# Three stage borders of a hybrid encoder layer: a GpSimd wait, a store on another queue, a regrouped gate product and a later awaited store

## What is computed

```
hn = rms_norm(h, norm_w);  proj = hn @ w_in          # qa ka va za, gates, qb kb vb zb, qc zc
qkv = silu(centred_depthwise_conv([qa, ka, va], conv_w_a)); qa, ka = l2_norm(qa), l2_norm(ka)
o_fwd = gated_delta_rule_chunked(qa, ka, va, g_f, bt_f)
o_bwd = flip(gated_delta_rule_chunked(flip(qa), flip(ka), flip(va), flip(g_b), flip(bt_b)))
o_a = rms_norm(o_fwd + o_bwd, o_norm_a) * silu(za)   # per head of 128
o_b = windowed_gqa_with_sink(rope(rms_norm(qb)), rope(rms_norm(kb)), vb, sink) * silu(zb)
o_c = memory_cross_attention(rms_norm(qc), rms_norm(km), vm) * silu(zc)
return h + concat(o_a, o_b, o_c) @ w_out
```

## Time and profile before

| | us |
|---|---|
| median of 3 runs | 2324.76 |
| lowest and highest of them | 2321.35, 2329.73 |
| profiled execution, its own time | 2328.26 |
| its span in the trace | 2326.6 |
| TensorE busy | 2164.2 (93% of the span) |
| VectorE, ScalarE, GpSimd busy | 1083.9, 660.8, 314.1 |
| front stage, until TensorE's last instruction in it | 1197.2 |
| delta stage, until the engines start the next | 1787.2 |
| attention stage, until SyncE's first load of the next | 1953.6 |
| output stage, until the end of the span | 2326.6 |
| mean granted TensorE clock | 0.97 of full speed |

### The profile page before, as it was taken

The page is one execution under the profiler, slowest core; times in us unless marked ns, Lnnn a source line. Parts: engine busy times, 40 slices in busy tenths (PEclk is TensorE's granted clock), DMA queues, the critical chain, the costliest instruction groups (busy, mean ns, idle before and its releaser), DMA issues. The chain is left out here.

```text
span 2326.6 us, 28431 instructions
## 1 busy us (share of the span) xinstructions
PE 2164.2 (93%) x11264; PEld 1807.5 (78%) x11264; DVE 1083.9 (47%) x1854; ACT 660.8 (28%) x1004; POOL 314.1 (13%) x195
## 2 busy tenths in 40 slices
PE   6999999999999999999967999999987785999998
PEld 6888888888888888888856888888885454888887
DVE  7764444444444311221318666666644876323222
ACT  6511111111111110111115454444433665211110
POOL 4300000000000000000005444455401000000000
PEclk9999999999999999999988999999979997999999
DMA  6522122122122212212121221111111125534432
GB/s 225 191 85 81 55 81 81 54 81 81 55 81 81 81 58 78 81 54 81 46 84 55 81 93 58 64 64 64 46 64 55 55 82 184 214 127 149 158 126 90
DMA packets 78866, 210.87 MB, mean 91 GB/s; under 512 B 7328, under 2 KB 33056, under 8 KB 74560
## 3 DMA queue, kind: packets, MB, share of 16 engines
q1 hardware_dynamic: 69088, 174.04, 22.5%
q0 software_dynamic: 9696, 35.72, 3.9%
HBM read 165.11 MB, written 44.63 MB: 90 GB/s over the span
## 5 line engine op out<-in xcount | busy, mean ns | idle before, releaser
L73 PE MATMUL pr_acc<-x_hi,pr_w_lo 128*128 128x512 f32 (+1 forms) x1760 | 675.8, 384 | 26.4 <-DVE pr_w_lo L431 20.7
L74 PE MATMUL pr_acc<-x_lo,pr_w_hi 128*128 128x512 f32 (+1 forms) x1760 | 674.1, 383 | 0.0
L75 PE MATMUL pr_acc<-x_hi,pr_w_hi 128*128 128x512 f32 (+1 forms) x1760 | 674.0, 383 | 0.0
L73 PEld LDWEIGHTS pr_acc<-x_hi,pr_w_lo 128*128 128x128 f32 x1760 | 334.0, 190 | 91.9 <-issue 18.7
L74 PEld LDWEIGHTS pr_acc<-x_lo,pr_w_hi 128*128 128x128 f32 x1760 | 334.1, 190 | 63.8 <-issue 0.2
L75 PEld LDWEIGHTS pr_acc<-x_hi,pr_w_hi 128*128 128x128 f32 x1760 | 334.1, 190 | 63.4
L347 ACT ACTIVATE pr_w_hi<-pr_w_raw 128x1024 fp32r<-128x1024 f32 x118 | 124.9, 1060 | 749.3 <-PE pr_acc L75 728.4
L532 DVE TENSOR_TENSOR pr_padded<-pr_acc,pr_rstd 128x512 f32<-128x512 f32 x82 | 56.6, 692 | 518.4 <-PE pr_acc L75 518.3
L73 PE MATMUL ou_acc<-ou_w_hi,ou_m_lo 128*128 128x512 f32 x512 | 200.5, 392 | 18.1 <-DVE ou_w_lo L1842 18.1
L74 PE MATMUL ou_acc<-ou_w_lo,ou_m_hi 128*128 128x512 f32 x512 | 200.4, 391 | 0.0
L75 PE MATMUL ou_acc<-ou_w_hi,ou_m_hi 128*128 128x512 f32 x512 | 200.1, 391 | 0.0
(11 more groups left out here) (240 smaller groups left out, 2508.1 us busy)
## 6 DMA issues: line engine op xcount, KB each, us to landing
pr_w_raw<-in_w_in SPq DMA_DIRECT2D x118, 512.0 KB, 5.1
ou_w_raw<-in_w_out SPq DMA_DIRECT2D x32, 1024.0 KB, 4.9
proj_scratch<-pr_res POOLq DMA_DIRECT2D x50, 512.0 KB, 5.2
dl_qk<-proj_scratch SPq DMA_DIRECT2D x8, 1024.0 KB, 5.0
dl_grow<-gate_rows SPq DMA_DIRECT2D x8, 1024.0 KB, 7.6
ou_x_in<-in_x SPq DMA_DIRECT2D x8, 1024.0 KB, 7.1
out<-ou_res POOLq DMA_DIRECT2D x8, 1024.0 KB, 4.7
pr_res<-in_x_t SPq DMA_DIRECT2D x11, 512.0 KB, 5.9
```

Of the source, the lines that this page charges most:

```text
L73: pe.matmul(out, w_lo, x_hi, start=first, stop=False)
L74: pe.matmul(out, w_hi, x_lo, start=False, stop=False)
L75: return pe.matmul(out, w_hi, x_hi, start=False, stop=last)
```

## The change

It has five parts.

1. GpSimd no longer issues the store of the last projection tile. SyncE does, after the two stores of gate rows; GpSimd waits only until that tile has been taken, then goes to the border.
2. In the delta stage GpSimd waits for `e_d1` of 4, VectorE's four products and sums of head 0 (L1129 and L1135), before `decayed_queries(0)`.
3. In the slot of head 7, ScalarE does the squares of the attention keys and of the first two tiles (`early_squares`) right after the squares of head 6, ahead of that head's roots. Before they came behind them.
4. After the delta stage's last exponential for the attention stage, ScalarE takes one logarithm of a single column into `negc`, which nobody reads.
5. For head 7, VectorE multiplies `po`, `onorm` and `z` as soon as the squares are taken (two operations), and the root is applied in one last operation. `fin` is now held across the stages, SyncE issues its store and does not wait for it; the wait (`stored` of 32) stands at the end of the attention stage.

```diff
@@ front_stage, SyncE
                 sp.dma_start(gate_rows[group], gate_sums[32 * group:32 * group + A_HEADS, :]).then_inc(g_st, 16)
+            sp.wait_ge(s_taken, TILES * 2)
+            sp.dma_start(proj[TILES - 1], res[:, 0]).then_inc(stored, 16)
             sp.wait_ge(g_st, 32)
@@ front_stage, GpSimd
                     if isinstance(first, int) and first + j == TILES - 1:
-                        pool.dma_start(proj[first + j], res[:, j % 2]).then_inc(stored, 16)
                         return
@@ delta_stage
-        osq, fin = n.sb("osq", [P, SEQ]), n.sb("fin", [P, SEQ])
+        osq, fin = n.sb("osq", [P, SEQ]), early["fin"]
@@ delta_stage, SyncE
             heads(slot)
-            store(A_HEADS - 1)
             sp.wait_ge(a_c, 16 * 13)
-            sp.wait_ge(f_st, 16 * A_HEADS)
+            sp.wait_ge(f_st, 16 * A_HEADS - 16)
+            sp.wait_ge(f_res, A_HEADS)
+            sp.dma_start(mixed[A_HEADS - 1], fin[:]).then_inc(stored, 16)
@@ delta_stage, ScalarE
+                act.activation(negc[:, 0, 0:1], c["one"][:, 0:1], ACT.Ln)
...
                 if before:
                     end_squares(h - 1)
+                if not more:
+                    early_squares()
@@ delta_stage, GpSimd
             neg_rows(0)
             pool.wait_ge(stored, 16)
+            pool.wait_ge(e_d1, 4)
             decayed_queries(0, 0)
@@ delta_stage, VectorE
             heads(slot)
-            end(A_HEADS - 1, 1)
+            f, parity = A_HEADS - 1, (A_HEADS - 1) % 2
+            dve.wait_ge(l_on, 16)
+            dve.wait_ge(l_z, f * 16 + 16)
+            dve.wait_ge(f_st, f * 16)
+            dve.wait_ge(f_sq, f * 2 + 2)
+            for half in range(2):
+                cols_ = bass.ts(half, HALF)
+                dve.scalar_tensor_tensor(fin[:, cols_], po[:, half], onorm[:, 0:1], z[:, parity, cols_],
+                                         ALU.mult, ALU.mult).then_inc(f_x, 1)
+            dve.wait_ge(f_x, f * 2 + 2)
+            dve.wait_ge(f_rc, f + 1)
+            dve.scalar_tensor_tensor(fin[:], fin[:], 0.5, osq[:], ALU.mult, ALU.mult).then_inc(f_res, 1)
@@ attention_stage, SyncE
             store(BLK - 1)
+            sp.wait_ge(stored, 32)
```

More of the change, by code:

```diff
@@ L827, in early_square, with early_squares @@
                 act.activation(root[:, i % 2], qk[:, i % 2], ACT.Square).then_inc(a_sq, 1)
-            def early_norms():
+            def early_squares():
                 act.wait_ge(a_k, 16)
@@ L836, in early_norms @@
                 early_square(1)
+            def early_norms():
                 for half in range(2):
@@ L1378, in _, with attention_stage @@
             end_sums(A_HEADS - 1, f_rt, 2 * (A_HEADS - 1))
-def attention_stage(nc, c, proj, early, mixed):
+def attention_stage(nc, c, proj, early, mixed, stored):
     BLK, W = SEQ // P, 3 * P
@@ L1942, in program @@
         early = {name: held.enter_context(nc.sbuf_tensor("e_" + name, shape, F32)) for name, shape in (
-            ("k_pad", [P, SEQ + 2 * P]), ("rq", [P, BLK, 12]), ("cos", [P, SEQ]), ("sin", [P, SEQ]),
+            ("fin", [P, SEQ]), ("k_pad", [P, SEQ + 2 * P]), ("rq", [P, BLK, 12]), ("cos", [P, SEQ]), ("sin", [P, SEQ]),
             ("window", [P, 3, 3 * P]), ("kvt", [P, 8, MEM_LEN]), ("q_in", [P, 2, 8, P]), ("qw", [P, 1]), ("kw", [P, 1]),
@@ L1946, in program @@
         delta_stage(nc, c, proj, gate_rows, cols, args, mixed, stored, kv_scratch, early)
-        attention_stage(nc, c, proj, early, mixed)
+        attention_stage(nc, c, proj, early, mixed, stored)
         held.close()
```

## The result

The changed kernel has a median of 2315.86 us (20 runs, 2312.99 to 2328.94), the kernel before, run beside it, 2330.91 us (20 runs, 2318.96 to 2337.26). The ratio is 0.995, with a 95% interval of 0.9933 to 0.9967: faster by 0.33 to 0.67%. (The ratio is not that of the two medians, which would be 0.9935.) The forecast of 2317.1 us lies 1.2 us from the median, but it was a forecast of 7.7 us less, and what came is 12 us by the ratio and 15 us by the medians. As the rest shows, the close hit is luck as much as working: the forecast set off from a base that was 6.2 us too low and took 3.7 us too much for part 1, and 9.0 us that it left out came off as well.

The account below looks back on a forecast made before the run. TensorE, busy 93% of the span, bounds it; only its stalls and low-clock stretches can be won. Terms 4.6 - 2.0 + 0.8 + 0.3 + 4.0 = 7.7 us off 2324.76 gave 2317.1 us; range 2311 to 2323.5 us.

Parts of the forecast that it names:

- The prediction's own sign of being wrong: Front stage's border: a GpSimd drain of some us without a store was listed as showing the prediction wrong.
- The low bound of 0: Front stage's border: no gain from moving the last store, if GpSimd's drain keeps its length without it.
- rival (b): Drain stays partly, stores delay SyncE's loads, or head 0's sums run at the lower clock: 2320.7 us; chance 0.33.
- bound of 4.4 us: Head 0: largest loss from GpSimd's wait, if the sums and `products_i` both run at the lower clock.
- Rival (a): Head 0: GpSimd's wait pays, giving 2307.8 us whole or 2313.1 us in a milder form; chance 0.12.
- VectorE's 7.3 us: Head 0: with GpSimd held back, VectorE's five operations end 7.3 us earlier, at 1236.4.
- its upper bound: Head 7's slot: squares ahead of roots gain at most 0.8 us, TensorE's wait of 0.81 us there.
- rival (c): Head 0: a new stall of about 6 us leaves the clock low, slower, 2334.1 us with ten batches; chance 0.07.

Follow-up runs that it names:

- e1_drain: The changed kernel with one GpSimd drain instruction added ahead of its wait for the last projection tile; median 2312.41 us.
- e2_best: Changed kernel plus early GpSimd drain, query-tile loads 2 to 5 before head 6's store, squares of tiles 2 and 3 between the key's logarithms; 2302.33 us.
- e2_best_no_wait: e2_best without GpSimd's wait for head 0's first blocks; median 2303.57 us.
- e1_no_wait: The changed kernel without GpSimd's wait for head 0's first blocks; median 2326.86 us.
- e2_squares_alone: The kernel before with only the early squares put ahead of the roots in head 7's slot; median 2330.55 us.
- e2_old_end: The changed kernel with head 7's end in the old order, its store still awaited in the attention; median 2319.65 us.
- e3_store_alone: The kernel before with only the front stage's last store moved to SyncE; median 2330.65 us.
- e1_after: The changed kernel itself, profiled and timed a second time; median 2315.13 us.
- e3_wait_alone: The kernel before with only GpSimd's wait for head 0's first blocks added; median 2323.38 us.
- e1_tiles: The changed kernel with the loads of query tiles 2 and 3 ahead of the store of head 6; median 2320.67 us.

## Why the prediction was right

**Part 1 failed.** The step was "Without the store the nearest row for a GpSimd drain is 0.391 us". That row has no transfer of GpSimd between it and the drain before it, and it covers the end of two fills of 0.20 us each; it was no neighbour. The drain went from 5.14 to 4.31 us and the part brought 0.9 us, not 4.6. The sentence "it follows the store issued just ahead of it" took the last transfer for the cause; most of it comes from what GpSimd had issued before, as e1_drain shows. The prediction's own sign of being wrong, a GpSimd drain of some us without a store, came. The low bound of 0 and rival (b) had a place for it.

**Part 2 right.** 2.0 us were forecast. From the release to `take_i` after has 51.05 us, before 49.07; over the traces with the wait the mean is 50.7 (seven, 49.7 to 51.6), over those without it 48.5 (six, 47.2 to 49.5): 2.2 us, of which 1.6 us are left at the squares of head 6 (means of H 486.7 and 485.0). The forecast's rows each came at the time that it gave. Only its bound of 4.4 us adds up delays that lie beside each other: the sums did run at the lower clock (3.42 us), and `take_i` still waited for `columns(1)` alone. Rival (a) said that the wait pays; by its mechanism, VectorE's 7.3 us, it doesn't. In the median it does, by 11 to 12 us in the two pairs that keep the wait of slot 7, for a reason that no rival held; in the pair without that wait (e2_best and e2_best_no_wait) it doesn't.

**Part 3 right**: 0.97 us, 0.8 forecast; a little over its upper bound, which was 0.8 too.

**Parts 4 and 5 right**: 4.0 us against 0.3 + 4.0; 1.5 for the order (1.4 forecast), 2.5 for the store and the logarithm (2.9 forecast), 0.24 of them the logarithm's by the rows of after and before (0.3 forecast).

**Missing in the sum: the clock in slot 7.** By its own terms the sum should have been -0.9 + 2.0 - 1.0 - 4.0 = -3.9 us, and the measured median moved by 15, the traced executions by 12.7. The rest is above all V, 39.3 to 30.3. The prediction had this in front of it: rival (c) names the wait of 5.93 us and the clock of 0.50 behind it, but feared a second such wait at head 0, and didn't ask how long the first one's low stretch lasts or whether the change moves it. Its fear for head 0 was unfounded: the gap of 6.24 us ahead of the first sums in after was followed by one slow batch (3.42 us for four) and then 2.08 us for sixteen.

**The base.** The forecast was set off from 2324.76 us; with 20 runs before stands at 2330.91. Had only the parts' 3.9 us come, after would have been at 2327. That 6.2 us in the base and 3.7 in part 1 were wrong the one way and 9.0 from the clock the other is why the forecast met the median.

What is open: what decides the length of the low stretch. In the nine traces with a wait of 5.4 us or more, the clock was low for 27.3 to 30.7 us where the wait ended 0.7 to 2.3 us after the fall (before, e1_no_wait, e2_squares_alone, e2_old_end, e3_store_alone), and for 10.2 us where it ended 2.5 to 3.0 us after it (after, e1_after, e1_drain, e3_wait_alone). That is a rule read from nine executions, not a cause shown; that the wait as a whole is the cause is shown, on both kernels, since the four traces without it have no low clock there. (They also have four loads and two squares earlier; moving two of the loads alone, in e1_tiles, left the low clock in place.) Why the groups of times differ between kernels that reach slot 7 at nearly the same time wasn't tried.

## What to carry to other kernels

Before costing a change of 1 or 2 us, look in the profile for a wait of TensorE with a low clock behind it: what it costs can vary by 10 us with a shift of 2 us elsewhere, so remove that wait first (here by four loads ahead of a store and two squares one step earlier, 20 us of median), and only then judge the small edits. As far as these traces show, a drain of GpSimd is costed by all the transfers that it issued since the last one, not only by the one just issued; put a drain of its own where the engine is idle anyway. And run the kernel before often enough to know its groups of times before taking a median of three as a base.

## What the runs showed of the hardware

- GpSimd's drain was longer the more transfers it had issued since its last one: with none 0.03 to 0.14 us (0.39 beside two fills of 0.20, 2.46 beside an operation of 2.35), with 8 in the output stage 0.72 us, with 52 in the front stage 4.31 us in each trace that has them, that is, 0.08 to 0.09 us for each; with a 53rd issued at the same moment 5.13 to 5.14 us. Putting the drain elsewhere moved the 4.31 us whole.
- The same wait of TensorE in slot 7 (5.5 to 6.1 us) with the same work behind it is followed by 10.2 or by 27 to 31 us at the lower clock, with 30 or 40 us for the same products. A wait of 2.3 us was followed by 27.3 us, and no wait by none, although the work holds eight batches of sums with one or two columns.
- ScalarE loads its table again between exponential and logarithm (1.28 us ahead of L865, just behind L864's exponential). The Trainium skill (ScalarE: Activation LUTs, section Table sets: the hidden batching unit) lists a set with both; in this program the trace doesn't agree.
